# Two-layer streaming trunk on one core: cached keys and values loaded from ScalarE's DMA queue instead of SyncE's

## What is computed

```
h = rmsnorm(x) * (1 + sc1) + sh1
q_r,k_r,v_r,z_r,q_a,k_a,v_a,m_r,m_a = split(h @ w_in)
yA = retention(q_r, k_r, v_r, state) * silu(z_r)          # 8 heads
yB = band_attend(rmsnorm(q_a), rmsnorm(k_a), v_a,
                 cache_attn_k, cache_attn_v, rel_bias)    # 8 heads
x  = x + g1 * ((sig(m_r) * yA @ w_br_ret + sig(m_a) * yB @ w_br_att) @ w_out)
x  = x + g2 * (relu(norm(x) @ w_up)^2 @ w_down)
```

## Time and profile before

| | us |
|---|---|
| median of 3 runs | 1945.87 |
| lowest and highest | 1944.68 and 1947.09 |
| the profiled execution, its own time | 1945.64 |
| its span, first to last instruction | 1943.9 |

### The profile page before, as it was taken

One profiled execution on the slowest core, in us unless ns is written; L12 is line 12 of the kernel. 1 busy time (PEld: TensorE's weight loads), 2 busy tenths in 40 slices (PEclk: granted clock), 3 DMA queues, 4 the chain that ended last, 5 costly groups with the idle time before them and its releaser, 6 DMA issues.

```text
span 1943.9 us, 34369 instructions
## 1 busy us (share of the span) xinstructions
PE 1830.5 (94%) x11834; PEld 1639.9 (84%) x11834; DVE 985.4 (51%) x1390; ACT 737.7 (38%) x1240; POOL 355.9 (18%) x440
## 2 busy tenths in 40 slices
PE   3799999999999989999989999999999999999998
PEld 2577777777999979999978777777789999899998
DVE  2345555555634366553344555555564334755333
ACT  2243443444523235442223444444453222544322
POOL 1133333333000030000020433333320001200000
PEclk8899999999999999999999999999999999999999
DMA  8286776676555553446536777667647465344442
GB/s 291 75 222 179 188 192 194 187 193 193 188 194 184 166 193 117 122 131 213 169 115 194 194 193 192 187 194 193 193 132 240 159 223 196 98 121 128 130 130 98
DMA packets 444443, 335.44 MB, mean 173 GB/s; under 512 B 150393, under 2 KB 403513, under 8 KB 444354
## 3 DMA queue, kind: packets, MB, share of 16 engines
q1 hardware_dynamic: 429152, 285.40, 50.2%
q0 software_dynamic: 12288, 43.65, 6.7%
q10 hardware_dynamic: 2914, 5.18, 0.7%
HBM read 307.40 MB, written 28.08 MB: 173 GB/s over the span
## 4 chain that ended last, share of the span: by engine, by line
PE 68%; issue 20%; DVE 5%; POOL 3%; DMA 2%; ACT 1%; SPq 0%; POOLq 0%; DVEq 0%; ACTq 0%
PE G L1344 46%; PE G L1368 12%; PE X L1478 6%; PE X L1304 2%; PE X L1391 2%; DVE wlo L925 1%; DMA raw<-in_w_out_dram 1%; DVE qk L1127 1%; POOL small L577 1%; DVE st L1088 1%; ACT prob L714 1%; DMA out_dram<-st 1%; POOL out_dram L503 1%; POOL prob L558 0%; DVE hlo L999 0%
## 5 line engine op out<-in xcount | busy, mean ns | idle before, releaser
L925 DVE TENSOR_TENSOR wlo<-raw,whi 128x1024 fp32r<-128x1024 f32 x369 | 478.8, 1298 | 658.8 <-ACT whi L649 658.0
L649 ACT ACTIVATE whi<-raw 128x1024 fp32r<-128x1024 f32 x369 | 390.9, 1060 | 802.9 <-PE G L1344 438.8
L1368 PE MATMUL G<-whi,hhi 128*128 128x512 f32 x832 | 341.6, 411 | 28.1 <-DVE hlo L999 13.3
L1368 PE MATMUL G<-wlo,hhi 128*128 128x512 f32 x832 | 329.4, 396 | 0.0
L1368 PE MATMUL G<-whi,hlo 128*128 128x512 f32 x832 | 328.8, 395 | 0.0
L1344 PE MATMUL G<-hhi,whi 128*128 128x384 f32 x768 | 261.1, 340 | 6.8 <-DVE hlo L999 6.6
L1344 PE MATMUL G<-hhi,wlo 128*128 128x384 f32 x768 | 257.1, 335 | 0.0
L1344 PE MATMUL G<-hlo,whi 128*128 128x384 f32 x768 | 256.8, 334 | 0.0
L1368 PEld LDWEIGHTS G<-whi,hhi 128*128 128x128 f32 x832 | 159.1, 191 | 77.0 <-issue 31.3
L1344 PE MATMUL G<-ysp,whi 128*128 128x384 f32 x768 | 198.0, 338 | 0.0
L1368 PEld LDWEIGHTS G<-wlo,hhi 128*128 128x128 f32 x832 | 158.8, 191 | 35.4
(11 more groups left out here) (186 smaller groups left out, 2363.4 us busy)
## 6 DMA issues: line engine op xcount, KB each, us to landing
raw<-in_w_in_dram SPq DMA_DIRECT2D x256, 128.0 KB
raw<-in_w_in_dram SPq DMA_DIRECT2D x128, 256.0 KB
ada_w<-in_w_ada_dram SPq DMA_DIRECT2D x64, 512.0 KB, 4.9
raw<-in_w_up_dram SPq DMA_DIRECT2D x64, 512.0 KB
raw<-in_w_down_dram SPq DMA_DIRECT2D x64, 512.0 KB
raw<-in_w_in_dram SPq DMA_DIRECT2D x49, 512.0 KB
kc<-in_cache_attn_k_dram SPq DMA_DIRECT2D x64, 256.0 KB, 5.9
vc<-in_cache_attn_v_dram SPq DMA_DIRECT2D x32, 512.0 KB, 8.4
```

The lines of the kernel that those rows point to most:

```text
L649: return a.activation(out, in_, ACT.Copy)
L925: v.tensor_tensor(wlo[:, j % SPLIT, :, :], raw[:, j % RAW, :, :], whi[:, j % SPLIT, :, :].bitcast(F32), ALU.subtract).then_inc(blk_split, 1)
L1368: ins = t.matmul(B[b][:, :], x[:, kp * WK + k, n * P:(n + 1) * P], w[:, k, :], start=first and k == 0 and x is hhi and w is w_hi, stop=las ...
```

## The change

The 4 key DMAs and the 2 value DMAs leave SyncE's list, with their waits. ScalarE gets two functions with the same DMAs and the same waits: `cached_keys` is called behind `high(c, 1)`, `cached_values` behind `high(c, 5)`. Semaphores, tiles, sizes and order between the DMAs of one tensor stay.

```diff
@@ SyncE @@
                 for j in range(4):
                     load(c, j, [pair_rows(l, j, h * DH + base, DH) for base in (C_QA, C_KA, C_QR, C_KR)], wide)
-                sp.wait_ge(ss_done, c.head)
-                for a in range(4):
-                    src = cache_attn_k[l:l + 1, :, :, bass.ds(h, 1), 32 * a:32 * a + 32]
-                    sp.dma_start(kc[32 * a:32 * a + 32, :, :].rearrange("j b (n i) -> j (b n) i", i=32),
-                                 src.rearrange("l b (n j) h i -> j (l b n h) i", j=32)).then_inc(kc_full, 16)
                 load(c, 4, [pair_rows(l, 0, h * DV + base, DV) for base in (C_VR, C_ZR)], wide)
...
                 for j in range(1, 4):
                     load(c, 4 + j, [pair_rows(l, j, h * DV + base, DV) for base in (C_VR, C_ZR)], wide)
-                sp.wait_ge(pv_done, c.head)
-                for t in range(2):
-                    src = cache_attn_v[l, :, t * P:(t + 1) * P, bass.ds(h, 1), :]
-                    sp.dma_start(vc[:, t, :, :], src.rearrange("b k h d -> k b (h d)")).then_inc(vc_full, 16)
@@ ScalarE @@
-        def head(c, h, prev):
+        def cached_keys(c, l, h):
+
+            act.wait_ge(ss_done, c.head)
+            for m in range(4):
+                src = cache_attn_k[l:l + 1, :, :, bass.ds(h, 1), 32 * m:32 * m + 32]
+                act.dma_start(kc[32 * m:32 * m + 32, :, :].rearrange("j b (n i) -> j (b n) i", i=32),
+                              src.rearrange("l b (n j) h i -> j (l b n h) i", j=32)).then_inc(kc_full, 16)
+
+        def cached_values(c, l, h):
+
+            act.wait_ge(pv_done, c.head)
+            for m in range(2):
+                src = cache_attn_v[l, :, m * P:(m + 1) * P, bass.ds(h, 1), :]
+                act.dma_start(vc[:, m, :, :], src.rearrange("b k h d -> k b (h d)")).then_inc(vc_full, 16)
+
+        def head(c, l, h, prev):
...
             high(c, 1)
+            cached_keys(c, l, h)
             high(c, 2)
             if prev is not None:
                 probabilities(c)
...
             high(c, 5)
+            cached_values(c, l, h)
             high(c, 6)
             high(c, 7)
...
             with cnt.turn(S_HEAD.adds) as c:
-                head(c, 0, None)
+                head(c, l, 0, None)
             with act.Fori(0, HEADS - 1) as h, cnt.turn(S_HEAD.adds) as c:
-                head(c, h + 1, h)
+                head(c, l, h + 1, h)
```

## The result

The changed kernel takes 2073.61 us (median, 2069.99 to 2081.45), the kernel before 1945.70: a ratio of **1.0662** (95% interval 1.0629 to 1.0695), 128 us slower. The forecast was slower, 1957 us, with 1976 at the end of the range: right in sign and too small by a factor of eleven. It had put more than half of its 11.3 us into turn 0; most of the loss came in the loop. The profiled execution took 2071.5 us, span 2069.8.

What follows compares the result with a forecast made beforehand. TensorE, busy 94% of the span, bounds the kernel, so only its waits count. Loop 2.8, turn 0 6.8 and clock 1.7 make 11.3 us on 1945.6, giving 1957 us; range 1946 to 1976.

Steps and rivals of the forecast that it cites:

- turn 0: First turn of each layer: key issues queue behind ScalarE's stores, last 8.0 us against 4.6 allowed; 3.4 us wait twice, 6.8 us.
- values free: Two value issues behind block 5's copy, 1.57 us, fall in ScalarE's idle time of over 3 us and cost nothing.
- keys in time: Keys land at 351.7 (356.1 at most), before VectorE wants them at 356.06, so their arrival costs nothing.
- the start of the issues ahead of the engine: ScalarE's sequencer starts the key issues at 341.0, before its copy of block 1 begins at 341.37.
- How late they may end: In the loop, four key issues may last 5.1 us; each microsecond beyond is one of TensorE's in each of 14 turns.
- How long they last: In the loop, four key issues take 4.8 us in most turns; mean wait 0.2 us, 2.8 us over 14 turns.
- worth nothing, since no one waits for what stands behind it: Freeing SyncE of the issues gains nothing: block 4, bias and blocks 5 to 7 only come earlier into buffers used later.
- The 10.10 of the earlier trace: Four key issues on SyncE in turn 1 of layer 1 took 10.10 us, the upper bound for their length.
- The sign named for being wrong: The prediction fails if TensorE idles over 0.5 us ahead of `va_tok` in most turns.
- the clock: Two new 3.4 us gaps of TensorE in turn 0 bring on the lower clock once, 1.7 us.
- a wait in every turn: Rival: bias and block 5 drag the loop's issues to 6.1 us or more; 1968 us, 1981 at 7 us; chance 0.23.
- No change: Rival: ScalarE's own queue does not hold it, four issues of 0.5 us end before block 2's copy; 1945.6 us; chance 0.19.

Runs made afterwards that it cites:

- the run without neighbours: The change with a small states load from turn 1 on, and SyncE's bias and blocks 5 to 7 waiting for landed keys: 1955.28 us, ratio 1.0049.
- keys alone: The change with only the key DMAs on ScalarE, the value DMAs back on SyncE: 2076.61 us, ratio 1.0666.

## Why the prediction was wrong

**Right: what bounds and what hides.** No gain from relieving SyncE; values free; keys in time (VectorE waited for them once, 0.7 us); the start of the issues ahead of the engine (341.0 in the turn read there, and 378.41 here, 0.21 before block 1's copy).

**Right: "How late they may end".** The slack of 5.1 us for the issues predicts the wait to a tenth: 11.10 - 5.1 = 6.0, measured 6.05. A little of this is luck: the start was 0.21 us ahead of block 1's copy, not 0.37, and ScalarE started again after 0.12 us, not 0.36, and the two nearly cancel. In turn 0 of layer 0 the issues took 11.82 us; less the 4.6 allowed there that is 7.2, measured 6.96 (TensorE's timeline, changed kernel):

```profile
121.48 0.80 PE L1376 MATMUL G<-whi,hhi 128*128 128x512 f32 x1 [6.96 <-DVE wlo L933]
```

**Wrong: "How long they last".** This is the step that failed. I took 4.8 us in the loop, nearest to turn 0's rows; they lasted 7.7 to 11.5 us, 9.9 on the mean. The figure alone is right, as the run without neighbours shows (4.5 on the mean). Three things around it were not. First, I let the states' load be mostly over, counting it at the full rate from its issue. It takes longer than that; the list of DMA issues of the kernel before had a median of 6.2 us from issue to landing:

```profile
st<-in_state_ret_dram POOLq DMA_DIRECT2D x32, 512.0 KB, 6.2
```

By that row the second of the two, issued at 338.15, lands about 344.4, in the middle of the keys' time. The 3.6 us of lead came from the turn I read as well, one whose TensorE and ScalarE were late by a low clock and GpSimd was not. Its load stands 3.99 us ahead of block 1's copy; in nine of the 14 turns of the loop it is only 1.5 to 2.2 (of the other five, three follow such a clock and two are turns 1), as in the very next turn (GpSimd's and ScalarE's timelines):

```profile
387.62 1.52 POOL L503 DMA_DIRECT2D st<-in_state_ret_dram  x2 [5.71 <-DMA out_dram<-st]
389.67 1.09 ACT L649 ACTIVATE whi<-raw 128x1024 fp32r<-128x1024 f32 x1
```

The change did not move this load (1.7 to 5.0 us ahead of block 1's copy now, 1.5 to 5.0 before); it moved the keys to where it is still in flight. Second, the bias stood in no term of the 4.8 us, and block 5 was counted as only partly ahead of the keys' end. Third, the line "worth nothing, since no one waits for what stands behind it" looked only for waits, not for what an earlier bias sets off: GpSimd's decay table comes forward into the keys. The runs put sizes to it: without the states 3.7 us less, without bias, block 5 and decay table 4.0 less. The 10.10 of the earlier trace rows, keys beside the states, was near to what came; I had it as an upper bound and gave it the tail. Each microsecond past the threshold was 14, so the cost of the mistake was steep: the mean wait was 67.6 / 14 = 4.8 us, where 0.2 was forecast, 64.8 us of the error. The sign named for being wrong, over 0.5 us idle ahead of `va_tok` in most turns, came in all 14 (2.4 to 6.3 us).

**Wrong: turn 0.** 8.0 us taken, 11.8 and 12.9 measured: 15.0 us of waits in place of 6.8. The stores were sized about right (4.6 + 2.7 = 7.3 with them alone): with bias, blocks 5 to 7 and decay table held back, the issues of turn 0 took 8.7 and 8.0 us (8.3 and 7.8 without neighbours in the loop). The missing 3 to 5 us go with the transfers held back there.

**Wrong: the clock.** 1.7 us forecast, 44.3 measured. I priced it by the 2.4 us gaps of the kernel before, which bring the lower level on in few turns. The new gap, beside the old one, does so in 13 of 14 turns: over ten microseconds behind it the granted clock is 0.67 to 0.84 on the mean, and 1.00 only in the turn with a gap of 2.62. Its length alone does not decide, as gaps of 2.43 and 2.98 had it too. The lower clock adds about half again to the 82.6 us of new waits. Where the wait at the outputs stays away the clock nearly stays: 0.981 over the span with the keys later in the list and 0.986 without neighbours, 0.960 with the change, 0.985 before.

**The rivals.** The second, a wait in every turn, was the one that came, beyond the 7 us of issue to which it was worked out; at 9.9 us, its own rule gives 4.8 x 14. No change fell. The Trainium skill (DMA: Bandwidth & Descriptors, Issuing engines are not separate DMA queues) says that the time to initiate a DMA is usually small next to the DMA itself. That is so for the value DMAs (about 0.5 us each, landing after 5.6) and for the long runs (2.0 to 2.9 us for four), not for four DMAs of 2048 runs: 9.9 us for the four, landing 7.1 after the issue of each. What that section says of the transfers, that those of all issuing engines interleave on the same 16 engines, agrees with the runs without neighbours and with the packets of the three queues above.

What was not tried: a turn 0 with the keys ahead of the stores; bias, block 5 and decay table one by one; and the clock's part was not separated by a run of its own, it is read off the busy times.

## What to carry to other kernels

Here a DMA issue was as long as its queue made it: with 2048 short runs a DMA it lasted until most of the runs ahead had been moved, 4.5 us for four with next to nothing beside them and 9.9 with the states, the bias, block 5 and the decay table on the same engines. Leave such DMAs with an engine that has nothing else to do, or put them where the next thing wanted is further away than the longest issue in the trace; compare the slack with the longest, not with the typical one, when each microsecond beyond counts once a turn. And ask of everything that stood behind the moved work what it will set off by coming earlier. Read the neighbours in several turns, and count them to their landing, not from their issue.

## What was not expected of the hardware

Four issues of 2048 runs of 128 bytes took 4.0 to 5.7 us with next to nothing beside them and up to 13.6 us beside others (keys alone, turn 0), from either queue at like lengths with like neighbours; the same bytes in 512 runs a DMA 2.0 to 2.9. Beside states and bias not one run of the keys moved for 3.9 us, and the fourth issue ended with 2837 of 8192 runs still to move. A second such DMA in a row was already held, for 1.8 to 5.4 us. TensorE's granted clock fell behind idle stretches of 6 us to a mean of 0.72 over ten microseconds, so that the products after the wait took nearly twice as long (2.07 against 1.05, 3.43 against 1.89).
